# First block's output product: seven products of quarters for tiles 1 to 7, weight sums on GpSimd

## What is computed

```python
y = jnp.concatenate([o_gla, o_gdn, o_diff], axis=-1) @ w_out[l]   # (256 x 2048) @ (2048 x 2048)
x = x + gate[:, None, :] * y
```

## Time and profile before

| | us |
|---|---|
| runs | 3434.14, 3436.14, 3432.41 |
| median | 3434.14 |
| profiled execution, first to last instruction (span) | 3419.8 |
| PE busy in it | 3148.4 (92%) |
| VectorE, ScalarE, GpSimd busy | 1497.6, 543.4, 900.9 |
| L664 (both output products), PE busy | 223.5 |

### The profile page before, as it was taken

The page is one execution under the profiler, slowest core; times in us unless marked ns, Lnnn a source line. Parts: engine busy times, 40 slices in busy tenths (PEclk is TensorE's granted clock), DMA queues, the critical chain, the costliest instruction groups (busy, mean ns, idle before and its releaser), DMA issues.

```text
span 3419.8 us, 67514 instructions
## 1 busy us (share of the span) xinstructions
PE 3148.4 (92%) x31278; PEld 2723.8 (80%) x31278; DVE 1497.6 (44%) x2300; ACT 543.4 (16%) x1011; POOL 900.9 (26%) x545
## 2 busy tenths in 40 slices
PE   5999999998999999999996888887899999999998
PEld 4877887877878888444785777677889999999998
DVE  4745365464447511333534666667334432113111
ACT  1012102020210211100002344333110000000001
POOL 1000000000000010000000121112447797777774
PEclk8998999998999999999997999999999999999999
DMA  7955387764336553333772000000436654444443
GB/s 275 409 219 197 133 328 280 307 247 172 124 136 255 200 194 123 148 148 141 264 296 112 8 9 10 7 7 6 159 126 232 237 217 162 167 170 161 161 163 109
DMA packets 52571, 582.97 MB, mean 170 GB/s; under 512 B 6931, under 2 KB 9297, under 8 KB 10433
## 3 DMA queue, kind: packets, MB, share of 16 engines
q1 hardware_dynamic: 34352, 465.06, 35.9%
q0 software_dynamic: 17936, 113.59, 8.6%
HBM read 576.52 MB, written 2.10 MB: 169 GB/s over the span
## 4 chain that ended last, share of the span: by engine, by line
PE 75%; DVE 10%; DMA 7%; ACT 3%; issue 3%; POOL 1%; SPq 0%; ACTq 0%; DVEq 0%; POOLq 0%
PE PS L1599 24%; PE PS L366 14%; PE PS L1548 10%; PE PS L664 6%; DMA ring<-in_w_second_dram 3%; DMA ring<-in_w_vec_dram 2%; PE PS L409 2%; PE PS L1767 1%; PE PS L1780 1%; PE PS L363 1%; DVE ring L201 1%; PE PS L1616 1%; DMA ring<-in_w_start_dram 1%; PE PS L1558 1%; PE PS L1812 1%
## 5 line engine op out<-in xcount | busy, mean ns | idle before, releaser
L366 PE MATMUL PS<-H,ring 128*128 128x256 f32 x2944 | 668.8, 386 | 7.0 <-ACT H L694 7.0
L366 PEld LDWEIGHTS PS<-H,ring 128*128 128x128 f32 x2944 | 562.1, 193 | 94.9 <-issue 17.6
L1548 PE MATMUL PS<-H,ring 128*128 128x256 f32 (+2 forms) x1344 | 403.1, 462 | 5.7 <-DMA ring<-in_w_second_dram 5.5
L1599 PE MATMUL PS<-H,ring 128*128 128x128 f32 x3424 | 404.0, 275 | 2.2 <-DMA ring<-in_w_second_dram 2.2
L1599 PEld LDWEIGHTS PS<-H,ring 128*128 128x128 f32 x3424 | 394.2, 192 | 3.0 <-DMA ring<-in_w_second_dram 2.6
L1548 PEld LDWEIGHTS PS<-H,ring 128*128 128x128 f32 (+1 forms) x1344 | 254.1, 190 | 155.0 <-issue 124.7
L2224 DVE TENSOR_TENSOR W<-W,PS 128x256 f32<-128x256 f32 x58 | 24.4, 421 | 679.9 <-ACT W L1925 679.8
L1599 PE MATMUL PS<-H,W 128*128 128x128 f32 x2624 | 316.5, 276 | 5.3 <-POOL W L1451 4.6
L1599 PEld LDWEIGHTS PS<-H,W 128*128 128x128 f32 x2624 | 305.3, 193 | 6.0 <-POOL W L1451 5.0
L319 POOL DMA_DIRECT2D ring<-in_w_vec_dram x75 | 39.8, 530 | 919.9 <-DVE ring L880 780.8
L1446 POOL TENSOR_TENSOR W<-ring 128x1024 f32<-128x1024 f32 (+1 forms) x74 | 179.6, 2427 | 264.6 <-PE PS L1599 147.9
(11 more groups left out here) (473 smaller groups left out, 4380.4 us busy)
## 6 DMA issues: line engine op xcount, KB each, us to landing
ring<-in_w_second_dram SPq DMA_DIRECT2D x121, 2048.0 KB, 7.7
ring<-in_w_first_dram SPq DMA_DIRECT2D x68, 2048.0 KB, 7.7
ring<-in_w_vec_dram POOLq DMA_DIRECT2D x75, 1024.0 KB, 7.6
ring<-in_w_start_dram SPq DMA_DIRECT2D x16, 2048.0 KB, 15.5
H<-in_w_vec_dram POOLq DMA_DIRECT2D x21, 1024.0 KB, 7.9
Pj<-in_w_aside_dram SPq DMA_DIRECT2D x8, 2048.0 KB, 11.2
ring<-in_w_second_dram SPq DMA_DIRECT2D x9, 1536.0 KB, 7.1
Pj<-in_x_dram SPq DMA_DIRECT2D x1, 2048.0 KB, 10.6
```

The lines of the kernel that those rows point to most:

```text
L366: mm = pe.matmul(PS[:, t % 2, half * T:(half + 1) * T], ring[:, t % 2, k, half * P:(half + 1) * P], hT[:, k, :], start=(k == 0), stop=(k = ...
L1548: mm = pe.matmul(PS[0:cols, bank(q, half), 0:width], ring[:, q % RING].rearrange("p k n -> p (k n)")[:, k * 2 * cols + half * cols:k * 2 * ...
L1599: mm = pe.matmul(regions(bank2, r), w[:, k * P:(k + 1) * P], m[:, k, :], start=(first and k == 0 and r // 4 not in opened), stop=(last and ...
```

## The change

For output tiles 1 to 7 of both layers the 32 matmuls give way to seven products r = 0, 1, 6, 4, 2, 3, 5 of 8 matmuls each (128 x 128 by 128 x 128 tokens), into eight regions of the same two banks. The weight tiles come to the ring in quarters. GpSimd makes four sums of quarters per tile: the first ("begun") in place in the ring once the tile is loaded, needed by product 4; the three others into S_out once the tile before is multiplied, needed by products 2, 3 and 5. In layer 0 GpSimd's loads of the vectors stand between the first sum and the other three: three (later two) of them per tile, `OUT_VEC`. In layer 1 the first sum of tile 1 goes ahead of the small loads of the second block, the rest behind them. VectorE makes four sums of hT (T_out) beside tile 0, and behind each tile 1 to 7 four additions, after a copy by ScalarE. Tile 0 is as before. Some semaphores are shared to make room for the new ones (`SAME`, left out below, as are the counts in PER_TURN).

```diff
@@ -42,6 +42,9 @@
 def chunk_of(i):
 
     return 32 + i if i < 16 else i - 16 if i < 64 else i - 64
+
+
+OUT_VEC = [3, 3, 3, 3, 2, 2, 2]
...
@@ -284,6 +287,35 @@
     opened = [S(f"open{n}_loaded") for n in range(RING)]
     aside = lambda i: Pj[:, 16 + 16 * (i % 2):32 + 16 * (i % 2), :].rearrange("p (c t) n -> p c t n", c=2)
     bank_of = lambda l, t: t if l == 0 and t < NSIDE else t % 2
+    blocks = lambda t: t.rearrange("p a b -> p (a b)")
+    T_out = blocks(Pj[:, 32:48, :]).rearrange("p (n k t) -> p n k t", n=4, t=P)
+    S_out = blocks(Pj[:, 48:60, :]).rearrange("p (n a) -> p n a", n=3)
+    c_out = [blocks(W[:, a:a + 2, :]).rearrange("p (r t) -> p r t", t=P) for a in (24, 26)]
+    half_of = lambda j, s: hT[:, 8 * j:8 * j + 8, s * P:s * P + P]
+
+    def quarter1(t, n):
+
+        return ring[:, t % 2].rearrange("p k n -> p (k n)")[:, 1024 * n:1024 * n + 1024]
+
+    def out_regions(n, a, b=None, by=1):
+
+        r = PS[:, 4 + 2 * (n % 2):6 + 2 * (n % 2), :].rearrange("p b (r t) -> p (b r) t", t=P)
+        return r[:, a, :] if b is None else r[:, a:b:by, :]
+
+    def out_sums(pool, l, n, begun):
+
+        t, sums = NIN + n, S("out_sum")
+        if begun:
+            pool.wait_ge(load[t % 2].sem, load[t % 2].at(l, 16 * (t // 2 + 1)))
+            sums.inc(pool.tensor_tensor(quarter1(t, 2), quarter1(t, 0), quarter1(t, 2), ALU.subtract))
+            return
+        pool.wait_ge(tiles_done.sem, tiles_done.at(l, t))
+        pool.wait_ge(sums.sem, sums.at(l, 4 * n - 3))
+        sums.inc(pool.tensor_tensor(S_out[:, 1], quarter1(t, 3), quarter1(t, 2), ALU.subtract))
+        pool.wait_ge(sums.sem, sums.at(l, 4 * n - 2))
+        sums.inc(pool.tensor_tensor(S_out[:, 0], S_out[:, 1], quarter1(t, 0), ALU.add))
+        sums.inc(pool.tensor_tensor(S_out[:, 2], quarter1(t, 1), S_out[:, 1], ALU.subtract))
+    B["out_sums"] = out_sums
 
     def sp_program(sp):
         for n in range(NMOD1):
@@ -313,14 +345,24 @@
             bring("wsm_loaded", wsm[:, :, 16:24], A["w_in"][l][:, DA:DA + 8].rearrange("(k p) n -> p k n", p=P))
         narrow_weights(0)
         bring("wlr_loaded", wlr, A["gla_w_lr"][0])
+        def half(l, i):
+            pool.wait_ge(vec_done.sem, vec_done.start + (-1 if i < 2 else i - 2 if l == 0 else max(i - 1, VEC0[1])))
+            half_loaded[half_place(i)].inc(pool.dma_start(half_slot(i), A["w_vec"][i]), 16)
+            if i == 20 and l < NL - 1:
+                pool.wait_ge(S("narrow").sem, S("narrow").at(l, 1))
+                narrow_weights(l + 1)
         for l in range(NL):
-            for i in range(VEC0[l], VEC0[l + 1]):
-                pool.wait_ge(vec_done.sem, vec_done.start + (-1 if i < 2 else i - 2 if l == 0 else max(i - 1, VEC0[1])))
-                half_loaded[half_place(i)].inc(pool.dma_start(half_slot(i), A["w_vec"][i]), 16)
-                if i == 20 and l < NL - 1:
-                    pool.wait_ge(S("narrow").sem, S("narrow").at(l, 1))
-                    narrow_weights(l + 1)
+            ahead = VEC0[1] - sum(OUT_VEC) + 3 if l == 0 else VEC0[2]
+            for i in range(VEC0[l], ahead):
+                half(l, i)
             if l < NL - 1:
+                pool.wait_ge(S("mix_ready").sem, S("mix_ready").at(l, 4))
+                for n in range(1, NOUT):
+                    out_sums(pool, l, n, True)
+                    for i in range(ahead, min(ahead + OUT_VEC[n - 1], VEC0[1])):
+                        half(l, i)
+                    ahead += OUT_VEC[n - 1]
+                    out_sums(pool, l, n, False)
                 pool.wait_ge(vec_done.sem, vec_done.start + VEC0[l + 1])
                 pool.dma_start(crow, A["cvecs"][l + 1].partition_broadcast(P)).then_inc(S("crow_loaded").sem, 16)
                 pool.wait_ge(S("mix_ready").sem, S("mix_ready").at(l, 4))
@@ -657,12 +699,28 @@
             t = NIN + n
             tile_ready(t)
             bank_free(t)
-            for half in range(2):
-                for k in range(KC):
-                    if n == 0 and half == 0 and k % 4 == 0:
-                        need(S("mix_ready"), k // 4 + 1)
-                    mm = pe.matmul(PS[:, 4 + 2 * (n % 2) + half, 0:T], ring[:, t % 2, k, half * P:(half + 1) * P], hT[:, k, :],
-                                   start=(k == 0), stop=(k == KC - 1))
+            if n == 0:
+                for half in range(2):
+                    for k in range(KC):
+                        if half == 0 and k % 4 == 0:
+                            need(S("mix_ready"), k // 4 + 1)
+                        mm = pe.matmul(PS[:, 4 + half, 0:T], ring[:, t % 2, k, half * P:(half + 1) * P], hT[:, k, :],
+                                       start=(k == 0), stop=(k == KC - 1))
+            else:
+                plan = {0: (quarter1(t, 0), half_of(0, 0), 0), 1: (quarter1(t, 1), half_of(1, 0), 0), 6: (quarter1(t, 3), T_out[:, 3], 0),
+                        4: (quarter1(t, 2), T_out[:, 2], 1), 2: (S_out[:, 1], T_out[:, 1], 2), 3: (S_out[:, 0], T_out[:, 0], 3),
+                        5: (S_out[:, 2], half_of(1, 1), 4)}
+                opened = set()
+                for r in (0, 1, 6, 4, 2, 3, 5):
+                    w, m, after = plan[r]
+                    if r == 6:
+                        need(S("out_t"), 1)
+                    if after:
+                        need(S("out_sum"), 4 * (n - 1) + after)
+                    for k in range(8):
+                        mm = pe.matmul(out_regions(n, r), w[:, k * P:(k + 1) * P], m[:, k, :], start=(k == 0 and r // 4 not in opened),
+                                       stop=(k == 7), skip_group_check=True)
+                        opened.add(r // 4)
             tiles_done.inc(mm)
             if n and l < NL - 1:
                 square_sums_next(pe, l, n - 1)
@@ -840,9 +898,16 @@
         need(S("o_ms"), 2)
         do(f(o_r[1], o_r[1], ACT.Sqrt), S("o_root"))
         tiles_to(32 * NIN)
+
+        def out_first(n):
+
+            if n:
+                need(tiles_done, NIN + n + 1)
+                do(f(c_out[n % 2][:, 3, :], out_regions(n, 0), ACT.Copy), S("out_first"))
         if l < NL - 1:
             for n in range(NOUT):
                 t = NIN + n
+                out_first(n)
                 need(evac[t % 2], t // 2 + 1)
                 do(f(W[:, 2 * n:2 * n + 2, :], xT[:, 2 * n:2 * n + 2, :], ACT.Square), S("x_sq"))
             act.wait_ge(S("crow_loaded").sem, 16)
@@ -1164,16 +1230,36 @@
             need(evac[0], NIN // 2)
             need(evac[1], NIN // 2 - (n < 3))
             do(v.tensor_tensor(hT[:, 4 * n:4 * n + 4, :], Pj[:, 4 * n:4 * n + 4, :], Pj[:, 32 + 4 * n:36 + 4 * n, :], ALU.mult), S("mix_ready"))
+        settle()
+        t1, t2, t3, t4 = [T_out[:, n] for n in range(4)]
+        do(v.tensor_tensor(t1, half_of(0, 1), half_of(0, 0), ALU.subtract))
+        do(v.tensor_tensor(t3, half_of(1, 1), half_of(0, 1), ALU.subtract))
+        settle()
+        do(v.tensor_tensor(t2, half_of(1, 1), t1, ALU.subtract))
+        settle()
+        do(v.tensor_tensor(t4, half_of(1, 0), t2, ALU.subtract), S("out_t"))
         for n in range(NOUT):
             t = NIN + n
             need(tiles_done, t + 1)
+            if n:
+                c = c_out[n % 2]
+                need(S("out_first"), n)
+                do(v.tensor_tensor(c[:, 0:4:3, :], c[:, 3, :].unsqueeze(1).to_broadcast([P, 2, P]), out_regions(n, 1, 3), ALU.add))
+                settle()
+                do(v.tensor_tensor(c[:, 1:3, :], c[:, 3, :].unsqueeze(1).to_broadcast([P, 2, P]), out_regions(n, 3, 5), ALU.add))
+                settle()
+                do(v.tensor_tensor(c[:, 3, :], c[:, 2, :], out_regions(n, 3), ALU.add))
+                settle()
+                do(v.tensor_tensor(c[:, 1:3, :], c[:, 1:3, :], out_regions(n, 5, 7), ALU.add))
+                settle()
             for half in range(2):
                 k = 2 * n + half
-                ins = stt(xT[:, k, :], PS[:, 4 + 2 * (n % 2) + half, 0:T], mod[:, 32 + k:33 + k], xT[:, k, :], ALU.mult, ALU.add)
+                got = blocks(c)[:, half * T:half * T + T] if n else PS[:, 4 + half, 0:T]
+                ins = stt(xT[:, k, :], got, mod[:, 32 + k:33 + k], xT[:, k, :], ALU.mult, ALU.add)
                 if half:
                     evac[t % 2].inc(ins)
             if l < NL - 1 and n < NOUT - 1:
-                vectors(3 if n < 4 else 2)
+                vectors(OUT_VEC[n])
             if l == NL - 1:
                 B["beside"]["dve"](v, n)
         if l < NL - 1:
@@ -1376,6 +1462,7 @@
         S("ctx_loaded").inc(pool.dma_start(craw, A["ctx_2"][0].rearrange("(t p) n -> p t n", p=P)), 16)
         S("rows_zero").inc(pool.memset(rows[2], 0.0))
         pool.wait_ge(S("rows_zero").sem, 1)
+        B["out_sums"](pool, NL - 1, 1, True)
         ld = S("vec_loaded")
 
         def bring(t, r, src, n, width=P):
@@ -1400,6 +1487,12 @@
         bring(3, U_CV - U_W0, A["conv_w_2"][0].rearrange("j (k p) -> (j k) p", p=P), 12)
```

(10 more changed lines are left out.)

3 lines of the change are left out of this document (1 added, 2 removed).

## The result

The changed kernel took 3472.08 us (median of 4 runs, 3468.19 to 3475.84), the kernel before on the same chip 3433.86 us (4 runs, 3432.41 to 3436.14): a ratio of 1.0112, 95% interval 1.0099 to 1.0126. It is slower by 38.2 us, where +29.1 was forecast; 3472 lies in the range of 3452 to 3482.

What follows compares the result with a forecast made beforehand. TensorE was taken to bound the output stage, with layer 0's sums queued behind VectorE after the change. Layer 0 +31.1 and layer 1 -2.0 gave +29.1: span 3448.9, plus 14.3, 3463.2 us; range 3452 to 3482.

Steps and rivals of the forecast that it cites:

- What bounds the kernel: Layer 0's output stage: TensorE alone bounds it, six turns of 14.68 us; seven products would save 1.31 us a tile if hidden.
- the order on GpSimd: Layer 0: three sums queue behind vector loads that wait for VectorE; PE waits; +25.8 us to T of tile 7.
- the clash of the earlier trace: VectorE vectors and GpSimd sums delay each other, 4.44 for 2.29 us and 4.30 for 2.35; tile 6 taken at 16.5.
- R1: Rival, faster: GpSimd's sums in time everywhere, if a group's last load issues by about 2.5 us after T; -11.9 us, chance 0.05.
- The clock: Layer 0, tiles 1 to 5: PE restarts at half rate after its wait; +0.85 us a turn, bounds 0 and 4.2.
- R3: Rival, slower still: the clock stays at 1.2 GHz after restarts in tiles 1 to 5; 3480 or 3493 us, chance 0.15.
- The tail of layer 0: Behind layer 0's last tile: exposed recombination +2.1 us and a later c row +3.2 us.
- Recombination: Behind the last tile: ScalarE copy and four VectorE additions, exposed; +2.1 us.
- The c row: Behind layer 0's last tile: its load is issued later, at 12.3 us, delaying the Silu; +3.2 us, bounds 0 and 5.
- Layer 1: Six tiles save 7.8 us; tile 1 +1.55, recombination +2.1, late VectorE scalings +2.2; in all -2.0 us.
- The base: Whole run: median 3434.14 us is 14.3 above the profiled span of 3419.8, taken as unchanged.

Runs made afterwards that it cites:

- the filled wait: Changed kernel plus twenty unused products on PE ahead of the wait for S_out[1] in tiles 1 to 5 of layer 0; 3479.21 us in one run.
- both kernels where the c row was on time: Changed kernel with sums of 8 columns, 3443.44 us; changed kernel with sums ahead of loads and layer 0 stage vectors of 128 columns, 3440.23 us.
- the layer 1 kernel: Changed kernel with layer 0 put back as in the kernel before, so the change stands in layer 1 alone; 3437.04 us, ratio 1.0008.

## Why the prediction was right, and where not

- **What bounds the kernel, and the order on GpSimd: right.** For tiles 2 to 4 the forecast had the sums start 10.65 us after T, PE idle about 5.1 us and turns of 20.5; the profile has 10.63 to 10.78, 4.86 to 5.01 and 20.56 to 20.93, and the releaser is the sum L314. Tiles 5, 6 and 7 came at 17.74, 16.43 and 13.37 (18.1, 16.5, 13.37). From the start of the stage to T of tile 7 it is +25.9 us, forecast +25.8; that this is so close is in part luck, as tiles 2 to 4 cost 18.1 instead of 17.4 and tiles 1 and 5 7.4 instead of 7.9. The experiment with the sums ahead confirmed the cause: it takes 20.9 us out of this stretch, against the changed kernel beside it.
- **That the order is the whole cause: not claimed, and not so.** The prediction used the clash of the earlier trace rows for tile 6 and the tail only, and R1 named in-time sums as the faster case, with an issue by 2.5 us after T as its condition. With the sums first no load stands ahead of them at all, and the stage is still 17 us longer than before: two vectors of three meet a sum, and the last sum of tile 3 ends 15.1 us after T, where R1 wanted 11.6. R1 as stated lacked this second condition.
- **The clock: right in kind.** Taken at 0.85 us a turn, measured 0.9 to 1.6 in tiles 2 to 4 by the filled wait; in tile 5, where 0.7 was added, the last product started 0.4 us after the last sum (709.14, 709.58). The clock did not stay down (R3): the square sums behind each tile took 1.03 us. What the prediction did not have is that the clock also fell behind shorter waits, and there not every time (below).
- **The tail of layer 0: right in mechanism, short by 1.8.** Recombination +2.1: measured 2.07 (3.86 against 1.79) and confirmed by tails of 12.04 in both kernels where the c row was on time. The c row: +3.2 forecast, 5.1 measured (17.11 - 9.97 - 2.07), just past the upper bound of 5. Its issue was 12.53 us after T of tile 6 (12.3 forecast); its landing took 9.6 us instead of 8.2, and the term took the one landing of the profile before as fixed, though the load had moved within the turn, to 1.0 us ahead of the next weight tile's load (740.33, 741.37).
- **Layer 1: near nothing, as forecast, but -0.3 instead of -2.0.** Each of six turns fell by 1.30 or 1.31 us, as forecast. Tile 1 cost 2.5 instead of 1.55: its last sum ended 13.9 us after T of tile 0 instead of 13.5, and the clock, which the step had not counted, gave the other 0.5 (the layer 1 kernel, at a clock of 1.00, has +2.05). The tail cost 4.98 instead of 4.3: VectorE was 1.97 us late (2.2 forecast), but the square sums for the root took 2.07 instead of 1.13 us, at a granted clock of 0.50:

```profile
1411.50:1414.50 3.00, 2.07 (x4) 1.17 (x4) 0.42 (x1) 1.57 (x5) 0.00 (x0) 0.50 1.02 437
```

  The same row behind tile 7 of before has 1.13 us at 1.00. A wait of 4.81 us ahead of it, made by the recombination and the scalings, was costed as a wait alone and not by what PE does after it. With sums of 8 columns the scalings started in time, the square sums took 1.13 us, and only the 2.07 of the recombination was left: so the sums of tile 7 beside VectorE are the cause of the rest, as the step had it.
- **The base: wrong in what it said, without harm.** "14.3 us around the span" was no such thing: 1.8 to 2.2 us lie around it in the later profiled executions. The first was an execution some 12 us quicker than the median. The difference was carried over unchanged, so the sum came out as if it had been made against the median.
- **Where the other 9 us are.** Forecast +29.1, stages +32.8, medians +38.2. The tail and layer 1 explain 3.5, the turns 0.1. The 5.4 besides are outside the two stages. The prediction put the unchanged code at nothing; nine comparisons out of nine have something there (1.4 to 17.0 us), and its cause is open.
